# Sixteen modulation units move from an expert layer to a convolution's input projection

## What is computed

```python
c_act = jax.nn.silu(c.astype(jnp.float32))
for i in range(DEPTH):
    mod = (c_act @ ada_w[i].astype(jnp.float32) + ada_b[i].astype(jnp.float32)).astype(x.dtype)
    sh1, sc1, g1, sh2, sc2, g2 = jnp.split(mod, 6, axis=-1)
    h = modulate(rms_norm(x, norm_mix_g[i]), sh1, sc1)
    # y: attention in layer 0, the Hyena mixer in layer 1
    x = x + g1[:, None, :] * y
    h = modulate(rms_norm(x, norm_ffn_g[i]), sh2, sc2)
    x = x + g2[:, None, :] * hier_moe(h, moe_wg[i], moe_bg[i], moe_we[i], moe_be[i],
                                      moe_w_gate[i], moe_w_up[i], moe_w_down[i])
```

## Time and profile before

| what | value |
|---|---|
| median of 3 runs | 3402.31 us (3402.11 to 3406.21) |
| profiled execution | 3403.95 us |
| its span | 3402.1 us, mean granted TensorE clock 0.945 |
| TensorE busy | 3053.4 us (90%) |
| VectorE busy | 2099.4 us (62%) |
| ScalarE busy | 1249.4 us (37%) |
| GpSimd busy | 419.0 us (12%) |

### The profile page before, as it was taken

One profiled execution on the slowest core, in us unless ns is written; L12 is line 12 of the kernel. 1 busy time (PEld: TensorE's weight loads), 2 busy tenths in 40 slices (PEclk: granted clock), 3 DMA queues, 4 the chain that ended last, 5 costly groups with the idle time before them and its releaser, 6 DMA issues. The chain is left out here.

```text
span 3402.1 us, 32478 instructions
## 1 busy us (share of the span) xinstructions
PE 3053.4 (90%) x12620; PEld 2351.9 (69%) x12620; DVE 2099.4 (62%) x2341; ACT 1249.4 (37%) x1402; POOL 419.0 (12%) x108
## 2 busy tenths in 40 slices
PE   3599788897977877999899999899989999989998
PEld 2333476665866665777787777788868778768887
DVE  6544669987878874799555664566224566446631
ACT  3224246763211113678322223444232222344431
POOL 1100100001400001000000000244420000014442
PEclk9779889998978888999899999899989999999999
DMA  4200549982200001699322222222223222222222
GB/s 194 100 13 0 198 160 412 416 322 76 98 22 19 17 22 60 230 343 379 117 95 75 81 93 87 87 98 89 99 90 113 75 74 99 87 83 92 97 99 81
DMA packets 88734, 424.23 MB, mean 125 GB/s; under 512 B 9827, under 2 KB 15075, under 8 KB 60444
## 3 DMA queue, kind: packets, MB, share of 16 engines
q1 hardware_dynamic: 82844, 380.49, 30.6%
q10 hardware_dynamic: 5760, 41.95, 3.1%
HBM read 420.30 MB, written 2.10 MB: 124 GB/s over the span
## 5 line engine op out<-in xcount | busy, mean ns | idle before, releaser
L220 PE MATMUL psum<-h_high,weights_low 128*128 128x512 f32 x1888 | 749.0, 397 | 27.9 <-DVE h_low L339 15.7
L221 PE MATMUL psum<-h_high,weights_high 128*128 128x512 f32 x1888 | 743.1, 394 | 0.0
L222 PE MATMUL psum<-h_low,weights_high 128*128 128x512 f32 x1888 | 742.6, 393 | 0.0
L183 POOL TENSOR_TENSOR weights_low<-weights_raw,weights_high 128x2048 fp32r<-128x2048 f32 x89 | 414.1, 4653 | 2490.3 <-ACT weights_high L179 2490.3
L179 ACT ACTIVATE weights_high<-weights_raw 128x2048 fp32r<-128x2048 f32 x167 | 319.7, 1914 | 826.4 <-PE psum L222 770.3
L220 PEld LDWEIGHTS psum<-h_high,weights_low 128*128 128x128 f32 x1888 | 359.9, 191 | 117.8 <-issue 41.7
L222 PEld LDWEIGHTS psum<-h_low,weights_high 128*128 128x128 f32 x1888 | 359.5, 190 | 76.3
L221 PEld LDWEIGHTS psum<-h_high,weights_high 128*128 128x128 f32 x1888 | 359.8, 191 | 75.7 <-issue 1.4
L339 DVE TENSOR_TENSOR weights_low<-weights_raw,weights_high 128x2048 fp32r<-128x2048 f32 x78 | 178.7, 2292 | 316.7 <-ACT weights_high L179 316.7
L1393 DVE TENSOR_TENSOR weights_low<-more_raw,weights_high 128x1024 fp32r<-128x1024 f32 x168 | 201.8, 1218 | 14.6 <-ACT weights_high L1012 9.5
L2408 DVE SCALAR_TENSOR_TENSOR ff_tiles<-psum,params,ff_tiles 128x510 f32<-128x510 f32 (+1 forms) x176 | 123.7, 744 | 135.0 <-ACT ff_tiles L2386 129.1
(11 more groups left out here) (419 smaller groups left out, 4794.4 us busy)
## 6 DMA issues: line engine op xcount, KB each, us to landing
weights_raw<-in_moe SPq DMA_DIRECT2D x168, 512.0 KB, 5.8
more_raw<-in_moe SPq DMA_DIRECT2D x168, 512.0 KB, 6.0
weights_raw<-in_w_mix SPq DMA_DIRECT2D x76, 1024.0 KB, 4.9
weights_raw<-in_w_ffn SPq DMA_DIRECT2D x66, 1024.0 KB, 4.8
mod_weights<-in_ada_w ACTq DMA_DIRECT2D x40, 1024.0 KB, 7.9
weights_raw<-in_hy_w_in SPq DMA_DIRECT2D x12, 1024.0 KB, 4.9
mod_weights<-in_ada_w SPq DMA_DIRECT2D x8, 1024.0 KB, 15.8
weights_raw<-in_mla_w_o SPq DMA_DIRECT2D x4, 1024.0 KB, 6.9
```

What stands on the lines that cost most here:

```text
L183: self.nc.gpsimd.tensor_tensor(self.low[:, g % 2, :], self.raw[:, g % 2, :], self.high[:, g % 2, :].bitcast(F32), ALU.subtract).then_inc(s ...
L220: nc.tensor.matmul(out, w[1], rhs[0], start=start, stop=False)
L221: nc.tensor.matmul(out, w[0], rhs[0], start=False, stop=False)
L222: return nc.tensor.matmul(out, w[0], rhs[1], start=False, stop=stop)
```

## The change

Layer 0's expert phase keeps the first 8 of layer 1's 24 modulation units. The other 16, as 32 half units of 512 KB, are done in the input projection: SP loads them, in turn with the weights, into two slots in the norm's buffer `m.F`, which is free after the norm; VectorE multiplies and sums three after each of units 0 to 9 and two after unit 10. c is loaded and put through Silu again there. The low parts of the weights, which GpSimd made in this phase, are made by VectorE: that of unit 1 after the norm, the others after each unit's convolution.

```diff
+MOD_MOE = 8
@@ phase_moe, ScalarE
-                if modulation is not None and 1 <= i <= MOD_UNITS:
+                if modulation is not None and 1 <= i <= MOD_MOE:
@@ phase_moe, VectorE
-                if modulation is not None and 2 <= i < MOD_UNITS + 2:
+                if modulation is not None and 2 <= i < MOD_MOE + 2:
...
-                dve.wait_ge(s.mod_read, MOD_UNITS)
-                modulation_gains(nc, link, m, 1)
+                dve.wait_ge(s.mod_read, MOD_MOE)
+                modulation_gains(nc, link, m, 1, 0, 2 * MOD_MOE)
@@ phase_hyena_in
+        mods = m.F[:, :, :].rearrange("p (a two) n -> p a (two n)", two=2)
+        mod_loaded, halves, first_mod = (s.mod_loaded_0, s.mod_loaded_1), 2 * (MOD_UNITS - MOD_MOE), MOD_UNITS + MOD_MOE
+
+        c_act = on_chip(nc, ctx, "c_act", [P, D], F32)
...
             sp.sem_clear(stale)
+            sp.dma_start(c_act[:, :], d.c).then_inc(s.c_here, 16)
...
-            ring.stream(sp, d.hy_w_in, n, following)
+            def half(k):
+                if k >= 2:
+                    sp.wait_ge(s.mod_read, k - 1)
+                sp.dma_start(mods[:, k % 2, :], d.ada_w[first_mod + k // 2, :, (k % 2) * D:(k % 2 + 1) * D])\
+                    .then_inc(mod_loaded[k % 2], 16)
+
+            def unit(u):
+                if u < n + 2:
+                    ring._load(sp, d.hy_w_in[u, :, :] if u < n else following[u - n, :, :])
+
+            unit(2)
+            sp.wait_ge(s.h_ready, KC)
+            half(0)
+            half(1)
+            unit(3)
+            for u in range(n):
+                unit(u + 4)
+                for k in range(3 * u + 2, min(3 * u + 5, halves)):
+                    half(k)
             sp.wait_ge(s.tables, 32)
...
-            ring.make_lows(pool, n)
...
+            act.wait_ge(s.c_here, 16)
+            nc.scalar.activation(c_act[:, :], c_act[:, :], ACT.Silu).then_inc(s.c_ready, 1)
             norm_act(nc, act, m, s, m.X, shift=m.mod[:, 48:48 + KC], ring=ring)
...
             link = Link(dve, s.v)
+            dve.wait_ge(s.c_ready, 1)
             norm_dve(nc, dve, m, s, link, m.X, m.gain[:, 1, 0, :])
+            ring.make_low_beside(dve)
             argument(0)
...
+                if u < n - 1:
+                    ring.make_low_beside(dve)
+                for k in range(3 * u, min(3 * u + 3, halves)):
+                    dve.wait_ge(mod_loaded[k % 2], 16 * (k // 2 + 1))
+                    t = 2 * first_mod + k
+                    nc.vector.scalar_tensor_tensor(mods[:, k % 2, :], mods[:, k % 2, :], 1.0, c_act[:, :], ALU.mult, ALU.mult,
+                                                   accum_out=m.mod[:, t:t + 1]).then_inc(s.mod_read, 1)
 
             over_units(dve, n, body, first=2, after=lambda u: argument(u + 1))
+            dve.wait_ge(s.mod_read, halves)
+            modulation_gains(nc, Link(dve, s.v, base + 4 * n), m, 1, 2 * MOD_MOE, MOD_TILES)
```

More of the change, by code:

```diff
@@ L1455, in phase_hyena_in @@
         block, s, stale = ph.open(ctx, *NORM_SEMS, "v", "read_out", "conv", "pads", "here", "tables", "fv",
-                                  "layer_sum", "arg", "sine")
+                                  "layer_sum", "arg", "sine",
+                                  "mod_read", "mod_loaded_0", "mod_loaded_1", "c_here", "c_ready")
         zT = on_chip(nc, ctx, "zT", [FILTER_EMB, S], F32)
@@ L2486, in build @@
                 moe_front(nc, part, m)
-                moe(0, d.hy_w_in, d.ada_w[MOD_UNITS:2 * MOD_UNITS, :, :])
+                moe(0, d.hy_w_in, d.ada_w[MOD_UNITS:MOD_UNITS + MOD_MOE, :, :])
         with ExitStack() as part:
```

## The result

The changed kernel takes 3429.07 us (median of 4 runs, 3424.27 to 3432.89), the kernel before 3403.05; the ratio is 1.0074, with a 95% interval of 1.0057 to 1.0092. On another chip it was 3429.53 against 3401.38, 1.0081 (1.0064 to 1.0098). So it is slower, by 26 and 28 us, or 0.7 to 0.8%, where 19 were forecast. The profiled execution of the first comparison took 3432.89 us, with a span of 3431.1.

A forecast was written before the change was run, and what follows sets the result against it. VectorE bounds layer 0's passes, TensorE layer 1's and the projection, where VectorE's chain would take over. −22.3 (passes) + 41.3 (projection) = +19.0 on 3403.95 gives 3423.0; that execution being 1.6 above the median, 3422, range 3403 to 3437.

The forecast's parts named there:

- Part 1: Layer 0's expert passes: 16 modulation units and their loads removed after passes 10 to 25, −22.3 us.
- the hiccup: Layer 1's expert passes: SP waits for norm rows, ScalarE idles 2.3 us; 1.6 counted as lost, added to the gain.
- Part 2: Projection's start: c's load and Silu cost 4.6 us, paid for by the low part leaving GpSimd; root net 0.
- the collision: Projection's norm: GpSimd's unit-1 low part beside VectorE's additions; first square to root 13.35 us, against 8.82 in the latents stage.
- Part 3: Each projection unit: VectorE waits for the third modulation half, so a unit takes 14.6 us against TensorE's 10.88.
- X: End of VectorE's low part in a projection unit; the third half lands at X + 6.4, VectorE is ready at X + 2.3.
- S(2): Start of unit 2's convolution in the projection, forecast at 861.2 on the old trace's axis.
- S(10): Start of unit 10's convolution in the projection, after eight units of 14.6 us, forecast at 978.0 on the old trace's axis.
- S(1): Start of unit 1's convolution in the projection, forecast at 840.4 on the old trace's axis.
- (a): Projection: halves arrive unhindered 3.4 us after issue, units of 13.0 us, total +3.0, 3405; chance 0.11.
- (b): Projection: the wait for each unit's third half is hidden, units stay within 10.88 us, −17.4, 3385; chance 0.11.
- (c): Projection transfers run one after another, units of 16.7 us, 3443; or layer 0's passes stay long for the DMA; chance 0.06.

The follow-up runs named there:

- experiment 5: Kernel before with only the projection's low parts moved from GpSimd to VectorE, all modulation left where it was: 3398.5 us against 3401.8, ratio 0.9989.
- experiment 3: Kernel before with the last 16 of layer 1's 24 modulation units left out, projection untouched: 3379.1 us, ratio 0.9922.
- experiment 2: Changed kernel with SP issuing each unit's third half ahead of the 1024 KB weight unit, still two slots: 3409.9 us, ratio 1.0016.

## Why the prediction was right, step by step

**Part 1** said −22.3 us; −22.3 and −22.2 came. The Silus of passes 10, 11 and 27:

```profile
579.30 0.38 ACT L1086 ACTIVATE norm_tiles<-psum 128x256 f32<-128x256 f32 x1 [0.26 <-PE psum L1191]
588.27 0.38 ACT L1086 ACTIVATE norm_tiles<-psum 128x256 f32<-128x256 f32 x1 [0.26 <-PE psum L1191]
...
727.88 0.38 ACT L1086 ACTIVATE norm_tiles<-psum 128x256 f32<-128x256 f32 x1 [0.26 <-PE psum L1191]
```

727.88 − 579.30 = 148.58 us, against 170.72 in the earlier trace rows; the forecast was 148.7. The Silus come 8.6 us apart, 9.2 at each fourth, as named. The 1.6 us of the hiccup, for which the forecast gives no working, were 150.34 − 148.58 = 1.8. There is luck in that: layer 1's stretch takes 149.9 to 151.0 us in the other profiles, 1.1 to 2.3 more than layer 0's without modulation.

**Part 2** said that c's load and Silu are paid for by the collision that goes away. The norm in the changed kernel:

```profile
765.02 1.06 ACT L1526 ACTIVATE c_act<-c_act 128x1024 f32<-128x1024 f32 x1 [27.31 <-DMA c_act<-in_c]
765.99 4.25 ACT L288 ACTIVATE norm_tiles<-x 128x512 f32<-128x512 f32 x8
768.01 4.67 DVE L317 TENSOR_TENSOR root<-root,norm_tiles 128x512 f32<-128x512 f32 x6
774.85 0.69 ACT L292 ACTIVATE root<-psum,consts 128x512 f32<-128x512 f32 x1 [1.52 <-PE psum L307]
```

The stage starts at 761.58, the root comes 13.27 us later, against 13.35 in the earlier trace rows. The first convolution step comes at 798.66, 37.1 us after the start; 37.2 was forecast. Six additions in one go, where the earlier trace rows had a pair of 5.66 us. That GpSimd's step is gone was enough for this (experiment 5, where the gap was still there), but it was not needed: in experiment 3 the step is still there, the gap is not, and the collision is gone too. The forecast credits the first cause alone.

**Part 3** said 14.6 us per unit. One unit, VectorE and SP:

```profile
890.43 2.29 DVE L339 TENSOR_TENSOR weights_low<-weights_raw,weights_high 128x2048 fp32r<-128x2048 f32 x1
892.64 1.21 DVE L1593 SCALAR_TENSOR_TENSOR norm_tiles<-norm_tiles,c_act 128x1024 f32<-128x1024 f32 x1
...
893.77 1.22 DVE L1593 SCALAR_TENSOR_TENSOR norm_tiles<-norm_tiles,c_act 128x1024 f32<-128x1024 f32 x1
...
900.26 1.23 DVE L1593 SCALAR_TENSOR_TENSOR norm_tiles<-norm_tiles,c_act 128x1024 f32<-128x1024 f32 x1 [5.26 <-DMA norm_tiles<-in_ada_w]
...
892.75 0.33 SPq L149 DMA_DIRECT2D weights_raw<-in_hy_w_in  x1
893.88 7.96 SPq L1483 DMA_DIRECT2D norm_tiles<-in_ada_w  x3
```

The steps are those of the forecast: the low part ends at 892.72 (its X), SP issues the unit at once and the half 1.1 us after that, VectorE reads two halves and waits for the third. Here it waits 5.26 us. The ten waits have a mean of 4.65 us, where X + 6.4 against X + 2.3 gave 4.1, and from S(2) to S(10) a unit took 15.1 us. The half arrived at X + 6.9 in the mean of ten, and at X + 8.0 once. All 32 halves took between 3.4 and 6.9 us from issue to landing:

```profile
DMA to landing us min/median/max: 3.4/5.3/6.9
```

The term that was mis-sized is the 1.3 us by which the half was to land behind the unit. In units 1 to 9 the unit ahead landed 5.1 us after its issue in the mean, where 4.9 were taken, and the third half landed 1.8 us behind it (1.1 to 3.1). Part of that error is in the reading of the rows. dft_inv was issued 0.64 us behind dft_fwd:

```profile
784.66 0.59 SPq L1470 DMA_DIRECT2D dft_fwd<-in_dft_fwd  x1
785.30 0.43 SPq L1471 DMA_DIRECT2D dft_inv<-in_dft_inv  x1
```

So the pair took 0.64 + 7.5 = 8.1 us from the first issue, 3.2 more than the 4.9 of a load alone and not 2.6, and half of that is 1.6 us. Why single halves took up to 3.1 us is not shown.

**The chain.** S(1) and S(2) were to come 57.9 and 78.7 us after the stage's start; they came at 57.7 and 78.7. S(10) was to come at 195.5 and came at 199.9, and the end at 210.2 and came at 214.1: the forecast's error in this stage arises in the eight waits between (8 × 0.55 = 4.4 us), and 0.5 us of it is made up behind them. TensorE's waits for the sine and the argument were put at 9 and 5 us; they were 8.5 and 5.6.

**The sum.** −22.3 + 45.2 = +22.9, or −22.2 + 43.4 = +21.2 in the second pair, against +19.0. By the forecast's own sum the time is 3402.31 + 19.0 = 3421.3, where it says 3422. The 7 us between 3422 and 3429 are thus 2 to 4 of late halves; of the rest, up to 4.7 can be the long convolutions' stretch, of which it stays open whether a part is the change's.

**The rivals.** (a), halves that land unhindered, is what experiment 2 made: its projection came to 198.5 us, where (a) gives 169.3 + 25.3 = 194.6. In the changed kernel itself it didn't happen. (b) gave 3385 for a change without the wait; the third slot ran at 3385.3. (c) wants the half 8.3 us after the unit's issue; it came 6.9 us after it in the mean and 8.0 once, so (c) was not the rule. Its other half, passes that stay long, did not happen (148.58 us). The Trainium skill's formula (page "DMA: Bandwidth & Descriptors", Anatomy of one DMA) would have put the total at about 3416, an estimate. The page gives it for transfers issued from GpSimd, and these came from SP. It has the pair landing 5.6 us after the unit's issue, where 6.9 were measured, and the rows of this stage, with 6.2, were nearer.

## What to carry to other kernels

Work that fits into an engine's idle time only fits if its data is there: count, for each load, the time between the moment its slot comes free and the moment its reader arrives, and compare it with a landing time of the same size in the same queue. Here 1.15 us stood against a landing of 5.2 to 6.9. If a round has more readers than slots, one of them waits a whole landing in every round; a slot more, or a reader less, removes it (3429 to 3385 or 3391 us). On one queue, the small load that someone waits for goes ahead of the large one that nobody waits for yet (14 to 16 us of this stage).

## What had not been expected

Two identical norms differed by 4.5 us because a gap of 0.47 us in VectorE's additions let a GpSimd instruction take its turn in front of the last one; the gap was in both profiles of before and in that of experiment 5, where no GpSimd step stands beside it and the two additions behind it took 1.49 us, not 5.66; in the other kernels it was not there. A stretch that the change does not touch took 445 or 450 us, in one kernel from one execution to the next, with a granted clock of 0.75 or 0.69 at its start and 0.87 or 0.81 around the end of the convolutions; that is a fifth of what this change moved, and comparing by stage kept it out.
